# Neighbourhood attention stage: head norm by ones products and a power on GpSimd, Silu by tanh, gating on GpSimd

## What is computed

```python
def rmsnorm(x, g):
    xf = x.astype(jnp.float32)
    xf = xf * lax.rsqrt(jnp.mean(xf * xf, axis=-1, keepdims=True) + EPS)
    return xf.astype(x.dtype) * g

def head_rmsnorm(x, g, n_heads):
    B, T, W = x.shape
    return rmsnorm(x.reshape(B, T, n_heads, W // n_heads), g.reshape(n_heads, -1)).reshape(B, T, W)
...
    na_l = neighbourhood_attention(nq_l, nk_l, nv_l, nk_c, nv_c, rpb, rows)

    def combine(o, na, z, dtype):
        g = head_rmsnorm(merge_heads(o), gla_norm, GLA_HEADS).astype(dtype)
        return (jnp.concatenate([g, merge_heads(na)], axis=-1) * jax.nn.silu(z)) @ w_out
```

## Time and profile before

| | |
|---|---|
| median of 3 runs | 3938.5 us (3937.6 to 3943.05) |
| the profiled execution | 3938.22 us |
| its span in the trace | 3936.0 us |
| PE busy over the span | 3848.5 us (98%) |
| stretch of the 32 slots | 1675.5 to 1872.7 us |
| PE, DVE, ACT, POOL busy in it | 182.60, 126.02, 118.35, 32.34 us |

### The profile page before, as it was taken

How to read it: one execution, slowest core, us unless ns; L and a number is a source line. 1 busy time by engine, 2 the same in 40 slices (tenths; PEclk the granted TensorE clock), 3 DMA queues, 4 the chain that set the end, 5 groups by cost and what they waited for, 6 DMA issues and landing times. The chain is left out here.

```text
span 3936.0 us, 47747 instructions
## 1 busy us (share of the span) xinstructions
PE 3848.5 (98%) x18002; PEld 2391.9 (61%) x18002; DVE 1828.7 (46%) x3898; ACT 974.7 (25%) x1833; POOL 885.4 (22%) x912
## 2 busy tenths in 40 slices
PE   8999999999999999989999999999999999999998
PEld 4688997776558568567444565655544444444447
DVE  3227885676343366656376222223556442313134
ACT  4224332333124311165234211111122100000000
POOL 0005774001111111111131112113132122222223
PEclk9999999999999999999999999999999999999999
DMA  5420003111211122162131112122244111111113
GB/s 197 152 91 10 9 9 69 42 48 54 86 43 63 51 65 71 55 208 79 49 116 53 50 41 72 47 76 96 84 146 147 56 39 47 43 43 43 43 48 102
DMA packets 119553, 279.57 MB, mean 71 GB/s; under 512 B 16859, under 2 KB 45835, under 8 KB 118304
## 3 DMA queue, kind: packets, MB, share of 16 engines
q1 hardware_dynamic: 112352, 261.19, 20.1%
q0 software_dynamic: 5920, 13.25, 1.4%
q10 hardware_dynamic: 1056, 2.10, 0.2%
HBM read 227.90 MB, written 50.87 MB: 71 GB/s over the span
## 5 line engine op out<-in xcount | busy, mean ns | idle before, releaser
L452 PE MATMUL upper_banks<-sbuf 128*128 128x512 f32 (+1 forms) x2016 | 771.3, 545 | 1.5 <-issue 1.1
L3379 PE MATMUL upper_banks<-sbuf 128*128 128x512 f32 x1400 | 617.1, 597 | 5.1 <-ACT sbuf L3656 3.5
L452 PEld LDWEIGHTS upper_banks<-sbuf 128*128 128x128 f32 x2016 | 382.4, 190 | 388.7 <-issue 372.8
L3379 PEld LDWEIGHTS upper_banks<-sbuf 128*128 128x128 f32 x1400 | 263.2, 191 | 317.8 <-issue 308.5
L2511 PE MATMUL gla_prod<-sbuf 128*128 128x512 f32 x560 | 247.6, 593 | 0.3 <-DVE sbuf L2550 0.3
L608 DVE TENSOR_TENSOR sbuf<-upper_banks,sbuf 128x512 f32<-128x512 f32 (+1 forms) x140 | 81.8, 584 | 283.2 <-PE upper_banks L452 282.7
L404 POOL TENSOR_TENSOR sbuf<-sbuf 128x512 f32<-128x512 f32 x36 | 47.5, 1320 | 655.2 <-DMA sbuf<-in_w_mlp_out 307.1
L1039 PE MATMUL mla_banks<-sbuf 128*128 128x128 f32 x1344 | 176.0, 278 | 5.9 <-POOL sbuf L878 4.7
L2511 PEld LDWEIGHTS gla_prod<-sbuf 128*128 128x128 f32 x560 | 103.6, 190 | 119.9 <-issue 117.4
L1662 PE MATMUL mls_banks<-sbuf 128*128 128x512 f32 x392 | 175.1, 593 | 0.3 <-DVE sbuf L2079 0.3
L1039 PEld LDWEIGHTS mla_banks<-sbuf 128*128 128x128 f32 x1344 | 162.9, 192 | 10.7 <-POOL sbuf L878 7.5
(11 more groups left out here) (562 smaller groups left out, 6508.7 us busy)
## 6 DMA issues: line engine op xcount, KB each, us to landing
sbuf<-in_l_w_in SPq DMA_DIRECT2D x59, 512.0 KB, 3.9
sbuf<-in_w_in SPq DMA_DIRECT2D x52, 512.0 KB, 4.3
sbuf<-in_w_mlp_out SPq DMA_DIRECT2D x40, 512.0 KB, 3.5
sbuf<-in_w_mlp_in SPq DMA_DIRECT2D x32, 512.0 KB, 3.5
sbuf<-in_l_w_mod SPq DMA_DIRECT2D x24, 512.0 KB, 6.2
scratch_gates<-sbuf SPq DMA_DIRECT2D x48, 256.0 KB, 2.0
sbuf<-in_na_bias SPq DMA_DIRECT2D x80, 128.0 KB, 2.9
sbuf<-in_l_w_mod SPq DMA_DIRECT2D x8, 1024.0 KB, 16.8
```

The source lines that it names most:

```text
L452: last = nc.tensor.matmul(bank_of(n, c)[:, 0:wd], lw[:, k * P:(k + 1) * P], right_operand(c, base, tw, k, o, wd, to), start=k == 0 and c i ...
L3379: last = nc.tensor.matmul(pb, lw[:, k * P:(k + 1) * P], rhs, start=k == 0 and c in ("P1", "P2", "P5"), stop=k == 3, skip_group_check=True)
```

## The change

The sums of squares come from products whose stationary operand is the full 128x128 `ones` and whose moving operand is the squares: 8 products of 512 columns leave each token's sum on all 128 partitions, so that nothing has to be spread later. DVE scales them out of PSUM into `root` with 4/128 and 4 eps (`sums_out`), and POOL raises `root` to -0.5, elementwise on 128x1024 (`inverse_root`); that is half the inverse root. Silu becomes `z + z tanh(z/2)`, twice the Silu: tanh on ACT, product and sum on POOL (`silu`). POOL multiplies `osum` by the gate and then by `root`; the norm weight goes into `zg` by an Identity with a scale on ACT (`norm_weight`) between the tanh and POOL's part. The half for `zn` is put into DVE's `outputs`. On ACT one step of this (a tanh or a norm weight) follows the exponentials in each of the steps 1 to 11. The tanh tiles lie in `H`, so its load moves from lead e = 6 to lead e = 10 and waits for `zn_up` 4 and `ygla` 4.

```diff
--- before.py
+++ after.py
-    NO, GATE0 = 8, 8
+    NO = 8
+    SUM_BANK = (6, 4, 6, 6)
+    Z_ORDER = [("zn", 0), ("zg", 0), ("zn", 1), ("zg", 1), ("zg", 2), ("zn", 2), ("zg", 3), ("zn", 3)]
+    Z_STEPS = [s for kind, j in Z_ORDER[1:] for s in ([("zg", j), ("gl", j)] if kind == "zg" else [("zn", j)])]
...
-        osq = [early[:, 3584 + j * NLAT:3584 + (j + 1) * NLAT] for j in range(3)] + [U[:, 5, NCTX:T]]
+        root = [U[:, 4 + j, NCTX:T] for j in range(4)]
+        tz = [H[:, r, NCTX:T] for r in range(8)]
...
-                    if p == 2:
+                    if p == 3:
+                        sp.wait_ge(zn_up, 4)
+                        sp.wait_ge(ygla, 4)
...
+            def silu(z, t, n):
+                pool.wait_ge(tanhed, n + 1)
+                nc.gpsimd.tensor_tensor(t, t, z, ALU.mult).then_inc(silued, 1)
+                pool.wait_ge(silued, n + 1)
+                return nc.gpsimd.tensor_tensor(z, t, z, ALU.add)
+
             def gate(j):
-                if j == 0:
-                    pool.wait_ge(zsil, 1)
-                nc.gpsimd.tensor_tensor(osum[:, j, :], osum[:, j, :], zg[j], ALU.mult).then_inc(ygla, 1)
+                pool.wait_ge(osqd, j + 1)
+                pool.wait_ge(gated, 2 * j + 1)
+                nc.gpsimd.tensor_tensor(osum[:, j, :], osum[:, j, :], zg[j], ALU.mult).then_inc(gated, 1)
+                pool.wait_ge(gated, 2 * j + 2)
+                pool.wait_ge(rooted1, j + 1)
+                nc.gpsimd.tensor_tensor(osum[:, j, :], osum[:, j, :], root[j], ALU.mult).then_inc(ygla, 1)
+
+            def inverse_root(j):
+                pool.wait_ge(scopied, j + 1)
+                nc.gpsimd.tensor_tensor(root[j], root[j], expo[:].broadcast_to([P, NLAT]), ALU.pow).then_inc(rooted1, 1)
 
...
-                pool.wait_ge(oev, 12 + 4 * k)
+                pool.wait_ge(ygla, k + 1)
...
-            for j in range(4):
-                gate(j)
+            for n, (kind, j) in enumerate(Z_ORDER):
+                if kind == "zn":
+                    silu(zn[:, j, :], tz[4 + j], n).then_inc(zn_up, 1)
+                else:
+                    silu(zg[j], tz[j], n).then_inc(gated, 1)
+                    inverse_root(j)
+                    gate(j)
...
-                for t in range(8):
-                    last = nc.tensor.matmul(banks[:, 7, 256 + 8 * j + t:257 + 8 * j + t], osq[j][:, t * P:(t + 1) * P], ones[:, 0:1],
-                                            start=True, stop=True)
+                if j >= 2:
+                    pe.wait_ge(scopied, 1 if j == 2 else 3)
+                for a in range(2):
+                    last = nc.tensor.matmul(banks[:, SUM_BANK[j] + a, :], ones[:], root[j][:, 512 * a:512 * a + 512], start=True, stop=True)
...
+                    if m == 0:
+                        pe.wait_ge(scopied, 2)
...
+                if i == 0:
+                    pe.wait_ge(scopied, 4)
                 B = banks[:, 6 + i % 2]
-                if 0 <= i - GATE0 < 16:
-                    pe.wait_ge(ginv, 1)
-                    for t in range(2):
-                        c = 2 * (i - GATE0) + t
-                        nc.tensor.matmul(B[:, (2 + t) * P:(3 + t) * P], gcol[:, c:c + 1].broadcast_to([P, P]), ident[:],
...
+            def tangent(kind, j):
+                z, t = (zn[:, j, :], tz[4 + j]) if kind == "zn" else (zg[j], tz[j])
+                if kind == "zg" and j == 0:
+                    act.wait_ge(zg_in, 64)
+                if kind == "zn":
+                    act.wait_ge(*((zn_in, 48) if j else (zn_first, 16)))
+                last = nc.scalar.activation(t, z, ACT.Tanh, scale=0.5)
+                if kind == "zn":
+                    last.then_inc(tanhed, 1)
+
+            def norm_weight(j):
+                if j == 0:
+                    act.wait_ge(gl_in, 16)
+                nc.scalar.activation(zg[j], zg[j], ACT.Identity, scale=gl[:, j:j + 1]).then_inc(tanhed, 1)
...
-                nc.scalar.activation(osq[j], osum[:, j, :], ACT.Square).then_inc(osqd, 1)
-            act.wait_ge(zn_first, 16)
-            nc.scalar.activation(zn[:, 0, :], zn[:, 0, :], ACT.Silu).then_inc(zn_up, 1)
+                nc.scalar.activation(root[j], osum[:, j, :], ACT.Square).then_inc(osqd, 1)
+            tangent("zn", 0)
...
-                if i == 1:
-                    act.wait_ge(zg_in, 64)
-                    for j in range(4):
-                        last = nc.scalar.activation(zg[j], zg[j], ACT.Silu)
-                    last.then_inc(zsil, 1)
-                if i == 4:
-                    act.wait_ge(zn_in, 48)
-                    for j in range(1, 4):
-                        last = nc.scalar.activation(zn[:, j, :], zn[:, j, :], ACT.Silu)
-                    last.then_inc(zn_up, 1)
-                    act.wait_ge(gcopied, 1)
-                    nc.scalar.activation(gcol[:], gcol[:], ACT.Sqrt, bias=eps, scale=1.0 / P).then_inc(grooted, 1)
+                if 1 <= i <= len(Z_STEPS):
+                    step, j = Z_STEPS[i - 1]
+                    if step == "gl":
+                        norm_weight(j)
+                    else:
+                        tangent(step, j)
...
-                if u == 0 and p < 2:
+                if u == 0:
                     dve.wait_ge(zn_up, p + 1)
                 uu = NA_UNITS[u][0]
                 to, B = zn[:, p, uu * P:(uu + 1) * P], banks[:, 6 + i % 2]
-                nc.vector.tensor_tensor(to, B[:, P:2 * P], to, ALU.mult)
-                if 0 <= i - GATE0 < 16:
-                    j, o = divmod(2 * (i - GATE0), 8)
-                    dve.wait_ge(ygla, j + 1)
-                    x = osum[:, j, o * P:(o + 2) * P]
-                    nc.vector.scalar_tensor_tensor(out=x, in0=x, scalar=gl[:, j:j + 1], in1=B[:, 2 * P:4 * P], op0=ALU.mult, op1=ALU.mult)
+                nc.vector.scalar_tensor_tensor(out=to, in0=to, scalar=0.5, in1=B[:, P:2 * P], op0=ALU.mult, op1=ALU.mult)
                 dve.drain()
                 nc.vector.tensor_tensor(to, B[:, 0:P], to, ALU.mult).then_inc(oev, 1)
 
+            def sums_out(j):
+                dve.wait_ge(osum1, j + 1)
+                for a in range(2):
+                    last = nc.vector.tensor_scalar(root[j][:, 512 * a:512 * a + 512], banks[:, SUM_BANK[j] + a, :], 4.0 / P, 4.0 * EPS,
+                                                   ALU.mult, ALU.add)
+                last.then_inc(scopied, 1)
+
             dve.wait_ge(cleared, 3)
+            sums_out(0)
             for i in range(-2, NS + 1):
                 if i + 2 < NS:
                     bias_max(i + 2)
+                if i <= 0:
+                    sums_out(3 + i)
                 if i >= 1:
                     outputs(i - 1)
-                if i == GATE0 - 1:
-                    dve.wait_ge(gl_in, 16)
-                    dve.wait_ge(grooted, 1)
-                    nc.vector.reciprocal(gcol[:], gcol[:]).then_inc(ginv, 1)
```

More of the change, by code:

```diff
@@ L4305, in na_block @@
         w_ready = [s.sem(f"w_ready{i}") for i in range(4)]
-        osqd, osum1, gcopied, grooted, ginv, zsil, zn_up, ygla = (
-            s.sem(c) for c in ("osqd", "osum1", "gcopied", "grooted", "ginv", "zsil", "zn_up", "ygla"))
+        osqd, osum1, scopied, rooted1, tanhed, silued, zn_up, gated, ygla = (
+            s.sem(c) for c in ("osqd", "osum1", "scopied", "rooted1", "tanhed", "silued", "zn_up", "gated", "ygla"))
         cleared = s.sem("cleared")
@@ L4407, in _ @@
             nc.gpsimd.memset(edge[:, :, :, 0:NCTX], 0.0).then_inc(cleared, 1)
+            nc.gpsimd.memset(expo[:], -0.5)
             pool.drain()
@@ L4591, in out_product @@
                         pe.wait_ge(oev, 3 * NU)
+                        pe.wait_ge(ygla, 4)
                     if p == 0 and c == "P2" and k == 3:
@@ L4757, in _ @@
                     bias_max(i + 2)
+                if i <= 0:
+                    sums_out(3 + i)
                 if i >= 1:
                     outputs(i - 1)
-                if i == GATE0 - 1:
-                    dve.wait_ge(gl_in, 16)
-                    dve.wait_ge(grooted, 1)
-                    nc.vector.reciprocal(gcol[:], gcol[:]).then_inc(ginv, 1)
-                if i == 0:
-                    dve.wait_ge(osum1, 4)
-                    nc.vector.tensor_copy(gcol[:], banks[:, 7, 256:288]).then_inc(gcopied, 1)
                 if 0 <= i + 1 < NS:
@@ L4789, in mix_end @@
             def mix_end():
+                dve.wait_ge(ygla, 4)
                 nc.vector.tensor_tensor(xt3[3], zn[:, 3, 512:1024], osum[:, 3, 512:1024], ALU.subtract).then_inc(mixed_end, 1)
```

2 lines of the change are left out of this document (1 added, 1 removed).

## The result

The kernel with the change takes **4550.66 us** (median of 4 runs, 4550.51 to 4553.16), the kernel before it 3940.78 us in the same series (4 runs, 3937.6 to 3944.09). The ratio is 1.155, with a 95% interval of 1.154 to 1.157: 610 us slower, where 3936 us was forecast with a range up to 3962. The profiled execution took 4553.16 us; its span is 4551.4.

A forecast was written before the change was run, and what follows sets the result against it. PE was taken to bound the kernel, busy 98% of the span; 2.2 us from spread products and nothing from the other terms gave 3938.2 - 2.2 = 3936 us, within 0.2%, range 3930 to 3962.

The forecast's parts named there:

- Spread products: Slots with PE's 32 spread matmuls: dropping them gains 8 pairs x 0.27 = 2.2 us, with 6.9 as the other end.
- Sums of squares and ACT: Early slots: new sums-of-squares products and Silu and root leaving ACT's batches cost or gain nothing, hidden before slot 5's bias.
- The wall of slot 5's bias: DVE at 1712.8 us: slot 5 waits for its bias to land from a full DMA queue, so earlier gains vanish.
- 4.1 us is the most that is to be had: Scores 3 to 7: without the wall they would take two pairs, 22.3 us, and not 26.4.
- P = 8: Length in us taken for one POOL power on 128x1024, the middle between 2.36 and 13.5; nothing late.
- the upper bound: POOL's power at most 13.5 us, from DVE's reciprocal costing 5.7 times a product per column, carried over to POOL.
- Rival 1: Power is long: from P = 13.4 every us costs 4; P = 20 gives 3962 us, P = 30 4002; chance 0.32.
- estimate of 10.2 us: POOL's power at 12 x 1024 cycles at 1.2 GHz; nothing late unless the bias is stuck behind H.
- 1755.8 + 4P: POOL's queue: time in us when zn 3 is ready, after 22 products and four powers of length P.
- The limit of 13.4 us: Power length under which slot 23's bias, behind H in SP's queue, is on time: 1755.8 + 4P < 1816.6 - 7.
- 8.8: Limit on P in us if slot 23's bias were stuck behind H's 4 MB, which takes 19.8 us to land.
- 3.7 to land: Landing time in us of slot 23's bias; with issues of H and bias it makes 7 behind zn 3.

The follow-up runs named there:

- the kernel with the product: Changed kernel with a POOL product in place of the power, so inverse root and norm left out: 3936.89 us against 3939.49 before, ratio 0.9994.
- the product with the early bias: Kernel with a product for the power, plus slot 5's bias issued ahead of the vectors and memory tokens: 3935.91 us (1 run) against 3939.94 before.
- the four Ln: ACT's batch where exp(-0.5 ln) replaced the changed kernel's power (3938.74 us); with slot 5's bias issued early too, 3936.86 us against 3940.34 before.
- the kernel with `H` behind the bias: Changed kernel with the power on 64 columns only, and H's load moved behind slot 23's bias: 3940.63 us, stage 197.11.
- the kernel with 128 columns: Changed kernel with the power on the first 128 of 1024 columns only, the rest unrooted: 3976.34 us, stage 239.2.
- the kernel with the power on 32 columns: Changed kernel with sums of squares in 32 columns, one 32-column power, PE's spread put back: 3941.27 us against 3938.4 before, ratio 1.0003.

## Why the prediction was wrong, point by point

**What bounds the kernel: right.** PE, in one stage of 197 us; the loss is PE's wait, DVE's queue being the link.

**Spread products, 2.2 us: right in size.** 2.0 us in slots 7 to 31 in the kernel with the product, and gone again with the spread put back on PE and DVE. That DVE's product has no part in it, as the prediction says, wasn't tested apart. The other end of 6.9 was no danger.

**Sums of squares and ACT, nothing: right, and for the reason given.** The wall of slot 5's bias was tested by taking it away. "4.1 us is the most that is to be had" came true as well: from scores 3 to 7 the product with the early bias takes 22.33 us, where 22.3 was written and before takes 26.4. Its 5.4 us against the product alone hold 1.4 us of early slots that were slower there than before (48.58 against 47.15). But with the wall gone ACT's batches do show, 2.1 us for the three Silu and 2.6 for the four Ln.

**POOL: the step that failed.** "On POOL that would be 13.5 us. I take P = 8." It is 163.2 us, 12 times the upper bound and 20 times the value taken. The bound carried a ratio over from DVE's reciprocal to another function on another engine. A ratio of 5.7 between a reciprocal and a product on DVE says nothing of a power on POOL, where it is 69. The text itself said that no row bounds this (Rival 1), yet it took P = 8 from this bound, held the 13.5 against Rival 1, and ended the range at P = 20. What the rows gave was a lower bound alone; the high end of the range should have been open.
The Trainium skill (GPSIMD Engine Reference, 3.1) gives about 12 cycles an element for code that branches on data, and the prediction's estimate of 10.2 us from that is 16 times too short for the power. Section 7 of the Trainium skill's GPSIMD Engine Reference prices a chain of dependent fp32 operations at 4 cycles an element; the prediction gave the chain no length. No run shows what the power's 0.159 us a column are made of.

**Rival 1, the mechanism: right with the measured price.** POOL's queue was given as zn 3 at 1755.8 + 4P; with P = 163.2 that is 2408.6, and the measured end is 2412.5, of which 2.5 us are the stage's later start. Waits at slots 8, 16 and 23, in that order, come out of the same formulas: zn 1 at 1718.0 + P = 1881 (measured 1885.2), zn 2 at 1741.6 + 3P = 2231 (2235.2). By Rival 1 the loss is 1755.8 + 4P + 7 - 1816.6 = 599 us. The bias of slot 23 is measured 611.6 later: 599, and 3.9 by which zn 3 is later than the formula, and 8.7 by which the bias comes 15.7 us and not 7 behind `H`. So nearly the whole of the miss is P, and 12.6 us are the stage's later start and the two queues.

**The limit of 13.4 us: wrong, and 8.8 was the nearer.** It lies between 9.3 and 10.5. The step that failed is "3.7 to land": that row is the median of twelve pieces, and only four of them were issued right behind `H`. By themselves those four took 12.9 us to land in the kernel before (above); the other eight took 3.3. Where the issue of `H` was late, the bias started 15.7 to 17.8 us behind it, in place of the 7. The case of a bias stuck behind `H` stood in the text, and its own test, the 12.9, lay in the trace, and the prediction doesn't use it.

**Chances.** 0.32 for slower came out of a price that was known from below only. Most of the chance at 3936 rested on P < 13.4, for which nothing spoke but the carried ratio.

## What to carry to other kernels

A function that no row of the trace shows has no upper bound from another engine's functions. Where such a price is multiplied by the count and stands in a queue, say at which price the forecast turns, and leave the range open above it, or measure one short instruction first (32 columns here would have told it: 5.45 us). At 0.159 us a column a power on GpSimd is for columns, not for tiles: root the sums before they are spread over a tile, or take exp(-0.5 ln) on ACT; either leaves this kernel's time as it was before. Before a large transfer is put ahead of small ones in a queue, price the small ones behind all of it, and don't take that price from a median that mixes them with others.

## What the runs showed of the hardware

- The power on GpSimd (fp32, SBUF to SBUF) takes 0.34 us and 0.159 us a column, on 128x1024 69 times a product. Exponents -0.5 and 2 cost the same, and so do 64 and 128 partitions.
- A bias of 128 KB a piece, issued behind one transfer of 4096 KB, was taken up by DVE 15.7, 15.8 and 17.8 us after the large one's issue. The four pieces right behind it land 12.9 us after their own issue in before, and 2.8 where they go ahead of it (the kernel with `H` behind the bias). The row of the issues in the kernel with 128 columns, 1838 to 1872 us (KB each, median us to landing):

```profile
sbuf<-in_na_bias SPq DMA_DIRECT2D x12, 128.0 KB, 12.1
```

- The granted clock falls about PE's wait ahead of slot 1. In before, where PE's last work is the products with one moving column, it is 0.72 from 1680 to 1682 us and 0.50 after it; in the kernel with the power on 32 columns, which has these products again, 0.62 and 0.50. The first scores start at 1675.56 and 1675.08 in these two. In the kernel with the product (1676.92), where PE's last work is the products of 512 columns, it falls 3 to 4 us later by the time from the first scores:

```profile
1682.00:1684.00 2.00, 0.33 (x1) 0.00 (x0) 0.94 (x3) 0.51 (x1) 1.42 (x1) 1.00 0.74 208
1684.00:1686.00 2.00, 0.00 (x0) 0.00 (x0) 1.84 (x6) 1.07 (x2) 1.92 (x2) 0.94 0.79 198
1686.00:1688.00 2.00, 1.95 (x10) 1.60 (x12) 1.35 (x3) 1.20 (x3) 1.38 (x1) 0.50 1.14 314
```

No kernel here beats the one before by more than its interval. The best stage, 191.1 us, leaves out the root. The kernel with the power on 32 columns, which has a root and no batch on ACT, was not run with the early bias.
